# A ring of eleven places for the expert weights, 4 MB transfers from expert 2 on, and a loop over experts written out

## The reference

```python
logits = xt @ w_router + b_router            # 32 experts, top 4 of them per token
gate = softmax(top_val)
hdn = xb @ w_mlp1[e] + b_mlp1[e]             # 1024 x 2048 per expert: 8 MB
act = glu * sigmoid(1.702 * glu) * (lin + 1) # both halves clipped at 7
y   = act @ w_mlp2[e] + b_mlp2[e]            # 1024 x 1024 per expert: 4 MB
```

## Time and profile before

| | before |
|---|---|
| median of 3 runs | 1125.36 us |
| the profiled execution | 1125.41 us |
| its span | 1123.6 us |
| PE busy | 1085.1 us, 97% |
| DMA engines, weight queue | 93.3% |
| HBM read | 437.67 MB, 390 GB/s over the span |
| 4 MB transfers | 43 + 29 |
| PE waiting for weights (matmul line L1154) | 6.3 + 4.9 us |

### The profile page before, as it was taken

How to read it: one execution, slowest core, us unless ns; L and a number is a source line. 1 busy time by engine, 2 the same in 40 slices (tenths; PEclk the granted TensorE clock), 3 DMA queues, 4 the chain that set the end, 5 groups by cost and what they waited for, 6 DMA issues and landing times.

```text
span 1123.6 us, 14458 instructions
## 1 busy us (share of the span) xinstructions
PE 1085.1 (97%) x5409; PEld 487.5 (43%) x5410; DVE 367.8 (33%) x813; ACT 245.6 (22%) x345; POOL 3.6 (0%) x12
## 2 busy tenths in 40 slices
PE   9999999999999999999999999999999999999996
PEld 8888888533333333333333333333333333333332
DVE  5977787422222222222222222222222222212223
ACT  4845674311111111111111111111111111111112
POOL 0000000000000000000000000000000000000000
PEclk9999999999999999999999999999999999999999
DMA  9655469999999999999999999999999999999996
GB/s 336 223 157 165 155 204 417 428 420 416 428 427 436 430 430 429 432 428 433 435 432 395 429 433 435 433 432 432 430 429 430 433 435 432 432 432 430 426 423 253
DMA packets 37877, 439.15 MB, mean 391 GB/s; under 512 B 5244, under 2 KB 5432, under 8 KB 21880
## 3 DMA queue, kind: packets, MB, share of 16 engines
q1 hardware_dynamic: 37488, 437.78, 93.3%
q10 hardware_dynamic: 360, 0.95, 0.3%
HBM read 437.67 MB, written 1.05 MB: 390 GB/s over the span
## 4 chain that ended last, share of the span: by engine, by line
PE 79%; DMA 14%; DVE 6%; issue 0%; ACT 0%; SPq 0%; DVEq 0%; PEldq 0%; ACTq 0%
PE bank L1154 33%; PE bank L1181 18%; DMA ring<-in_w_mlp_dram 11%; PE bank L798 9%; DMA late_slots<-in_w_mlp_dram 4%; PE bank L1083 3%; PE bank L1165 2%; PE bank L792 2%; PE bank L963 2%; PE bank L1011 2%; DVE xn L1670 2%; DVE xn L1667 2%; DVE xn L1674 2%; PE bank L1059 1%; PE bank L1067 1%; PE bank L1133 1%
## 5 line engine op out<-in xcount | busy, mean ns | idle before, releaser
L1154 PE MATMUL bank<-ring,xn 128*64 128x512 f32 x1232 | 276.3, 595 | 6.3 <-DMA ring<-in_w_mlp_dram 6.3
L1154 PE MATMUL bank<-late_slots,xn 128*64 128x512 f32 x880 | 197.5, 596 | 4.9 <-DMA late_slots<-in_w_mlp_dram 4.9
L1154 PEld LDWEIGHTS bank<-ring,xn 128*64 128x64 f32 x1232 | 84.4, 136 | 163.8 <-issue 150.3
L1181 PE MATMUL bank<-ring,smo 128*64 128x512 f32 x624 | 138.3, 595 | 0.0
L705 ACT ACTIVATE xn<-bank 128x512 f32<-128x512 f32 x33 | 19.7, 598 | 481.5 <-PE bank L1154 481.5
L1154 PEld LDWEIGHTS bank<-late_slots,xn 128*64 128x64 f32 x880 | 60.2, 136 | 117.9 <-issue 106.3
L1683 DVE SCALAR_TENSOR_TENSOR moe_y_lo<-bank,st,moe_y_hi 128x512 fp32r<-128x512 f32 x33 | 24.8, 750 | 235.5 <-ACT moe_y_hi L712 235.5
L1667 DVE TENSOR_SCALAR xn<-bank 128x512 f32<-128x512 f32 x33 | 22.8, 691 | 220.9 <-PE bank L1154 220.9
L1181 PE MATMUL bank<-late_slots,smo 128*64 128x512 f32 x416 | 92.1, 595 | 0.0
L1181 PEld LDWEIGHTS bank<-ring,smo 128*64 128x64 f32 x624 | 42.9, 137 | 81.1 <-issue 81.1
L712 ACT ACTIVATE moe_y_hi<-bank,st 128x512 fp32r<-128x512 f32 x33 | 22.7, 687 | 233.7 <-PE bank L1181 233.7
(11 more groups left out here) (270 smaller groups left out, 890.9 us busy)
## 6 DMA issues: line engine op xcount, KB each, us to landing
ring<-in_w_mlp_dram SPq DMA_DIRECT2D x43, 4096.0 KB, 30.4
late_slots<-in_w_mlp_dram SPq DMA_DIRECT2D x29, 4096.0 KB, 28.0
ring<-in_w_mlp_dram SPq DMA_DIRECT2D x28, 2048.0 KB, 13.4
late_slots<-in_w_mlp_dram SPq DMA_DIRECT2D x15, 2048.0 KB, 15.6
ring<-in_w_in_dram SPq DMA_DIRECT2D x22, 1024.0 KB, 5.4
late_slots<-in_w_mlp_dram SPq DMA_DIRECT2D x8, 1024.0 KB, 38.5
ring<-in_w_branch_dram SPq DMA_DIRECT2D x4, 1024.0 KB, 5.0
ring<-in_w_out_dram SPq DMA_DIRECT2D x4, 1024.0 KB, 7.1
```

Of the source, the lines that this page charges most:

```text
L1154: last = mm(B[4 + u][g * C:(g + 1) * C, :], xgT[:, k % 4, k // 4, :], by_group(held[k // 2][0][:, k % 2, u * FF:(u + 1) * FF], g), start=F ...
L1181: last = mm(B[7][g * C:(g + 1) * C, :], actT[:, j, h * C:(h + 1) * C], held[4 + h][0][:, j // 2, (j % 2) * D + g * N:(j % 2) * D + (g + 1) ...
```

## The change

The ring has 11 places, chunk m goes to place m % 11, and none is used once. The eleventh is where `place_used_once` was; `smo` moves behind `sga` and `sgm` so that it adjoins the late slots. Two chunks go as one 4 MB transfer when their places adjoin, which is so for all even m but those with m % 11 equal to 3 or 9, from expert 2 to expert 29. The rounds are gone: SP's and PE's code has one stretch per expert. The first eleven chunks are issued at the same points as before, in another order. Chunks 3 and 5 of expert 31 come as 1 MB + 0.5 MB + 0.5 MB, and PE waits for the last 0.5 MB only before the matmuls that use it. The final scalings are put in another order. The weight of the final norm is read into another place and issued one chunk later.

```diff
-PLACES = 10
-ROUND = PLACES // 2
-QUADS = range(ROUND + 1, E - 2)
+FIRST_QUADS = 2
+PLACES = 11
+QUADS = [m for m in range(CHUNKS * FIRST_QUADS, CHUNKS * (E - 2), 2) if m % PLACES not in (3, PLACES - 2)]
...
-        late_pair = [late[:, 2 * i:2 * i + 2, :] for i in range(4)]
-        places = [late_pair[1], pair[0], pair[1], pair[4], pair[5], pair[2], pair[3], late_pair[2], late_pair[3], late_pair[0]]
+        late_pair = [late[:, 2 * i:2 * i + 2, :] for i in range(5)]
+        places = late_pair[1:5] + pair + late_pair[0:1]
+        quads = {n: late[:, at:at + 4, :] for n, at in ((PLACES - 1, 0), (0, 2), (1, 4), (2, 6))}
+        quads.update({4 + n: ring[:, 2 * n:2 * n + 4, :] for n in range(5)})
...
                 if pieces == 2:
-                    for half, done in enumerate((place_landed[place], piece_landed[i])):
-                        sp.dma_start(places[place][:, half, :], src[:, half * SLOT:(half + 1) * SLOT]).then_inc(done, 16)
+                    at = [0, SLOT, 2 * SLOT] if i % 2 == 0 else [0, SLOT, SLOT + FF, 2 * SLOT]
+                    for a, b, done in zip(at, at[1:], (place_landed[place], piece_landed[i], half_landed.get(i))):
+                        sp.dma_start(places[place].rearrange("p a n -> p (a n)")[:, a:b], src[:, a:b]).then_inc(done, 16)
...
             sp.wait_ge(p_turned, AH)
-            load(0, 0, 0)
+            first_load(0)
             sp.wait_ge(slots_used, Q_BRANCH + 2)
-            load(0, 1, 1)
-            load(0, 4, 4)
+            first_load(4)
+            first_load(9)
             sp.wait_ge(slots_used, Q_OUT)
-            load(0, 2, 2)
-            load(0, 3, 3)
+            first_load(5)
+            first_load(8)
             sp.wait_ge(mg_turned, 2 * TT)
-            load(0, 5, None)
+            first_load(3)
             sp.wait_ge(slots_used, Q_OUT + 2)
-            load(1, 0, 5)
-            load(1, 2, 7)
+            first_load(1)
+            first_load(6)
             sp.wait_ge(slots_used, Q_MOE)
-            load(1, 1, 6)
-            load(1, 3, 8)
-            load(1, 4, 9)
+            first_load(2)
+            first_load(7)
+            first_load(10)
...
-            for e in range(1, ROUND + 1):
-                refill(e, e, CHUNKS, e + 2 in QUADS, e + 1 in QUADS)
-            with sp.Fori(1, E // ROUND - 1) as r:
-                for c in range(1, ROUND + 1):
-                    refill(r * ROUND + c, c, CHUNKS, True, True)
...
+            for e in range(E - 1):
+                after = sp.value_load(first_item[0:1, e + 1:e + 2], min_val=1, max_val=ITEMS - 1)
+                for i in range(CHUNKS):
+                    m = CHUNKS * e + i + PLACES
+                    if m >= CHUNKS * E:
+                        continue
+                    if m not in QUADS and m - 1 not in QUADS:
                         wait_freed(after, i)
+                        load(m // CHUNKS, m % CHUNKS, m % PLACES, 2 if m >= CHUNKS * (E - 1) + 2 else 1)
+                    elif m - 1 in QUADS:
                         wait_freed(after, i)
+                        load_quad(m // CHUNKS, m % CHUNKS // 2, (m - 1) % PLACES)
             after = sp.value_load(first_item[0:1, E - 1:E], min_val=1, max_val=ITEMS - 1)
-            wait_freed(after, 2)
+            wait_freed(after, 3)
...
+                        if u and k == KB - 1 and 3 in in_halves:
+                            pe.wait_ge(*in_halves[3])
...
+                        if j == 3 and 4 + h in in_halves:
+                            pe.wait_ge(*in_halves[4 + h])
...
-            experts(0, chunks)
-            pe.wait_ge(opened, 2 * TT)
-            scatter_b2()
-            with pe.Fori(1, (E - 2) // ROUND) as r:
-                experts(r, lambda c: chunks_in_round(c, r))
-            with pe.Fori(last_first, items) as i:
+            after = after_first
+            for e in range(1, E - 1):
+                if e == E // 2:
+                    pe.wait_ge(opened, 2 * TT)
+                    scatter_b2()
+                first = after
+                after = pe.value_load(first_item[0:1, e + 1:e + 2], min_val=1, max_val=ITEMS - 1)
+                with pe.Fori(first, after) as i:
+                    item(i, chunks(e))
+            with pe.Fori(after, items) as i:
...
-            final_scale(0)
+            final_rstd(0)
+            final_half(0, 0)
             final_mean(1)
-            final_scale(1)
+            final_half(0, 1)
+            final_rstd(1)
+            final_half(1, 0)
+            final_half(1, 1)
```

More of the change, by code:

```diff
@@ L115, in landings @@
     for m in range(CHUNKS * E):
[L116 to L121, removed]
+        place = m % PLACES
+        if m - 1 in QUADS:
             table.append(table[-1])
@@ L158, in build @@
         xhi_at = late_at
[L159 removed]
+        late = nc.alloc_sbuf_tensor_at("late_slots", [P, 2 * HALF + 2, SLOT], F32, offset=late_at)
         xhi_room = sb("xhi_room", [P, KB, S])
@@ L1101, in chunks, with item @@
             def chunks(e):
[L1103 to L1122, removed]
+                at = [(m, *landing[m]) for m in range(CHUNKS * e, CHUNKS * (e + 1))]
+                return [(places[m % PLACES], place_landed[place], 16 * count) for m, place, count in at]
             def by_group(columns, g):
                 return columns.rearrange("p (q g s) -> p g q s", g=2, s=ROWS)[:, g]
-            def item(i, held, in_pieces={}):
+            def item(i, held, in_pieces={}, in_halves={}):
                 pe.wait_ge(row_ready, i + 1)
@@ L1184, in item @@
                     last.then_inc(slots_used, 2)
+            items = pe.value_load(first_item[0:1, E:E + 1], min_val=1, max_val=ITEMS - 1)
             with pe.Fori(0, after_first) as i:
-                item(i, [(places[n], place_landed[n], 16) for n in range(CHUNKS - 1)] + [(once[:, :, :], once_landed, 16)])
-            last_first = pe.value_load(first_item[0:1, E - 1:E], min_val=1, max_val=ITEMS - 1)
-            items = pe.value_load(first_item[0:1, E:E + 1], min_val=1, max_val=ITEMS - 1)
-            def experts(r, held):
-                after = pe.value_load(first_item[0:1, bass.ds(r * ROUND + 1, 1)], min_val=1, max_val=ITEMS - 1)
-                for c in range(1, ROUND + 1):
-                    first = after
-                    after = pe.value_load(first_item[0:1, bass.ds(r * ROUND + (c + 1), 1)], min_val=1, max_val=ITEMS - 1)
-                    with pe.Fori(first, after) as i:
-                        item(i, held(c))
-            experts(0, chunks)
-            pe.wait_ge(opened, 2 * TT)
-            scatter_b2()
-            with pe.Fori(1, (E - 2) // ROUND) as r:
-                experts(r, lambda c: chunks_in_round(c, r))
-            with pe.Fori(last_first, items) as i:
-                item(i, chunks(E - 1), {c: (piece_landed[c], 16 * (SLOTS[:Q_MOE].count(c - 2) + 1)) for c in piece_landed})
+                item(i, chunks(0))
+            after = after_first
[8 more added lines that the diff above has]
+            with pe.Fori(after, items) as i:
+                item(i, chunks(E - 1), {c: (piece_landed[c], 16 * (SLOTS[:Q_MOE].count(c - 2) + 1)) for c in piece_landed},
+                     {3: (half_landed[3], 16 * (SLOTS[:Q_MOE].count(4) + 1)), 5: (half_landed[5], 16 * (SLOTS[:Q_MOE].count(5) + 1))})
             pe.wait_ge(gT_ready, items + 1)
@@ L1696, in final_scale, with final_half @@
                 dve.wait_ge(rstd, 2 * TT + t + 1)
-                for n in range(2):
-                    cut = slice(n * N, (n + 1) * N)
-                    v.scalar_tensor_tensor(out=xn[:, t, cut], in0=B[2 * t + n][:, :], scalar=st[:, 6 + t:7 + t],
-                                           in1=wfin[:, cut], op0=ALU.mult, op1=ALU.mult).then_inc(normed, 1)
+            def final_half(t, n):
+                cut = slice(n * N, (n + 1) * N)
+                v.scalar_tensor_tensor(out=xn[:, t, cut], in0=B[2 * t + n][:, :], scalar=st[:, 6 + t:7 + t],
+                                       in1=wfin[:, cut], op0=ALU.mult, op1=ALU.mult).then_inc(normed, 1)
             dve.wait_ge(s_small2, 16)
```

39 lines of the change are left out of this document (16 added, 23 removed).

## The result

The changed kernel takes 1129.17 us (median of 8 runs, 1128.16 to 1131.54); the kernel before, run beside it, 1125.36 us (8 runs, 1124.67 to 1126.95). The ratio is 1.0035, 95% interval 1.0026 to 1.0044: it is slower. The forecast was 1126.4, no difference that can be told.

The account below looks back on a forecast made before the run. The weight queue's landings up to chunk 189, then a fixed tail, were taken to bound the kernel. Landings 2.2 - 0.8 + 0.6 + 0.2 = +2.2 and tail -1.2 gave +1.0 on 1125.41: 1126.4 us, range 1123.6 to 1128.9.

Parts of the forecast that it names:

- What bounds the kernel: Weight queue sets the end: landing of chunk 189's last piece, then a fixed tail of PE and DVE work.
- Code written out: PE code from 507 to 1101: 22 more blocks, three full rounds of eight plus part of a fourth, +2.2 us.
- My own check from the front: Landings summed from the first quad at 240.1, plus 6.3 for blocks and 0.3 for edges: 1103.5 against 1101.0.
- Slower: the blocks go on the same engines: Rival, weights' queue: dearer blocks or last round complete before 1101; +3.6 us, 1129.0, chance 0.2.
- 4 MB from expert 2 on: Early weight transfers: first quad lands at 240.1, +0.6 us; four more pairs of singles, +0.2.
- My bound for an empty queue: First quad: with an empty queue a quad lands 12.3 us after its issue, so 240.6 at most.
- Ring of eleven: One more chunk in flight from expert 1 on: -0.8 us near 250, 0 at the expert with two items.
- Half pieces: Tail, expert 31's chunk 3: four passes run while the last 0.5 MB lands, -0.9 us.
- final scalings: Tail: DVE's 0.42 us wait for the square root goes, second half's mean moves to the middle, -0.3 us.
- the cover that I named: Expert 31's tail: chunk 5's last quarter is needed 0.3 us after landing; if late, 0.5 at most is given back.
- The blocks are hidden: Rival: added code blocks delay no landing; -1.5 us, 1123.9, chance 0.2.
- The ring fills a real gap: Rival: slice 22's dip to 395 GB/s was lost time, 2.3 us come back; 1124.1, chance 0.08.

Follow-up runs that it names:

- the new end with the old code: Kernel before with only the half pieces and the new order of the final scalings: 1124.89 us, ratio 0.9995.
- two experiments: PE's code alone written out on the kernel before, 1130.0 us; 4 MB transfers from expert 6 on, on the changed kernel, 1130.17 us.
- the second profile of the same kernel: The changed kernel run again without edit, beside the kernel before on another chip: 1128.59 us, ratio 1.003.
- the kernel with less code: Kernel before with the new tail and 28 fewer PE instructions (7 warming matmuls of 512 columns for 14 of 256): 1123.82 us, ratio 0.9984.

## Why the prediction was wrong, step by step

*What bounds the kernel*: right. The landing of chunk 189's last piece and the tail behind it give the whole difference of the two profiles, +4.1 - 1.3.

*Code written out* (+2.2, ends 0 and +4.5) is **the step that failed**, and by its size. The blocks came as counted: 22 in 507 to 1101, one about every 27 us. I counted the rounds wrongly. I let the fourth be "a part", 0.6 us, since it would be complete "only around 1095, just before chunk 189 lands"; just before is before, and the block at 1097.7 cost its whole 1.2 us on the second half of chunk 188, right ahead of 189. My own check from the front shows the size: it had 6.3 us for blocks and 0.3 for edges, 6.6 together, and 7.7 were measured; with a whole fourth round (1.5) it would have been 7.5. The written-out PE code alone makes the landing +3.0 and the time +4.7 (1130.0 against 1125.25, ratio 1.0038), where I took +2.2.

The rival *Slower: the blocks go on the same engines* had the condition "or the last round is complete before 1101" and the price 1129.0, at a chance of 0.2. The condition came true, for PE's blocks; of SP's blocks nothing was seen. That its price agrees with the median to 0.2 us is in part luck: it stands for landings +4.8, measured +4.1, and the median lies 1.0 above the profiled execution.

*4 MB from expert 2 on* (+0.8): the first quad landed at 240.7 where I had 240.1; the miss is 0.6. My bound for an empty queue, 12.3 us, was not that: the quad of 600.91 was issued 2.6 us before the one ahead of it landed, at 603.5. The first quad of the changed kernel, issued 1.4 us before the landing ahead of it (230.1), landed 10.7 us after that landing, not 9.72. The pairs of singles cost 0.4 and not 0.2. A line that I read over plays a small part: PE's read of `items` moved ahead of expert 0, so PE's first weight matmul starts at 216.14 in place of 215.66, and at 215.83 with the read put back.

*Ring of eleven* (-0.8 near 250): a gain of that size isn't there. The 0.8 us of before stood around a block fetched at 251.1, and I took it for a queue that ran short. In the changed kernel the queue is fuller there (435 GB/s over 246 to 262 us, against 393), a block comes at 251.2 all the same, and the landing at 261.7 is late by 1.4. The 0.8 isn't even a fixed property of the old ring: kernels with the same ring and code are 2.2, 1.0, 2.0, 0.8 and 0.3 us over plain prices from chunk 13's landing to chunk 21's (the kernel before, then the new end with the old code and with less, PE's code all and half written out). Over the whole chain PE's written-out code with ten places is 7.9 over, the changed kernel with eleven 7.7: 0.2 is left for the place. Zero at the two-item expert was right.

The parts then add up without a rest. From before to changed the landing of the first quad gives +1.2 (240.7 against chunk 13's 239.5), five pairs more as singles +0.4, and what is over plain prices 7.7 - 5.2 = +2.5: together +4.1. Forecast for the same three were +0.6, +0.2 and 2.2 - 0.8 = +1.4. Behind 555 us alone the changed kernel is 4.7 over plain prices, the kernel before 1.4, and the pairs of singles add 0.7.

*Half pieces* and *final scalings* (-1.2): right, -1.3. From the last piece to the end of PE's last pass on chunk 189 it is 1102.61 + 3.68 - 1105.11 = 1.2 us, before 1101.01 + 1.96 - 1100.97 = 2.0; so -0.8 for -0.9 predicted. The 32 passes on chunks 4 and 5 run unbroken in 7.04 us: the cover that I named held. Half a us is from the last scalings, 0.3 predicted.

*The blocks are hidden* and *The ring fills a real gap* fell. The rule of the Trainium skill ("Runtime: NRT & Kernel Launch", Instruction fetch mechanics), by which crossing into the next block is mostly hidden and a written-out loop is preferred, agrees with the trace for the engine that fetches: items keep their 26.77 us in code that runs for the first time. For the kernel it doesn't hold: writing out PE's code alone is 0.38% slower. Two rows of the chain of waits of the changed kernel:

```profile
817.13 7.04 PE bank L1127 x32
843.90 7.04 PE bank L1127 x32
```

*Not in the prediction*: what a late landing does to PE's clock. The sum took each us of landing as a us of time. With waits of 2.0 to 3.2 us the granted clock often fell to its lower level for 3.4 or 6.8 us. In two experiments this, with starts that were late already, made PE the bound and put more time between landing and end: 24.2 us with the old end (22.6 before, so +1.6) and 24.7 with the new one (21.3, so +3.4). Before, no wait for weights was longer than 1.4 us and none had a fall behind it. In the changed kernel's profiled execution one fall came, behind 2.52 us at 1013, and it was made up by the next wait for weights. Nor did the sum have the distance from the profiled execution to the median: 0.05 us before, 1.0 changed. Where that comes from is open.

## What to carry to other kernels

In a kernel that its weight queue bounds, count the 16 KB blocks of code that come in during the bound stretch. Here the loop that repeats its code has none, and written-out code pays some 1.5 us for each eight (7.7 us over plain prices for 33 blocks), most of it in one step. A block that comes after a long stretch without any pays a full step alone (1.2 us at 1098 before, 1.1 at 1101 with the new end); so where the last one falls can matter, and 28 instructions fewer ahead moved it from 1101.0 to 1110.2, behind the last transfer that counts. With the new end this was the one version here that beats both kernels (by 0.16%; without the 28 the ratio was 0.9995, and the two intervals just overlap). When a sum puts an event "just before" the instant that sets the end, count it whole.

## What the runs showed of the hardware

The cost of code blocks comes mostly in steps: in the changed kernel's profile seven of eight blocks move no landing by more than 0.2 us, the eighth by 1.2 to 1.4, with the steps 195 to 225 us apart; with PE's code alone written out the last three are 206 us apart. In the second profile of the same kernel the same blocks cost 1.0 to 1.1 and another of each eight costs 0.4, 1.5 per eight in all. It fits that the blocks go round the engines; which engine each one hit was not tested by an experiment. With half of the code written out, and with 4 MB transfers from expert 6 on, the steps are less clean (0.4 to 1.0), and the kernel with less code has one of 2.1 without a block, so the rule is not exact.

TensorE's granted clock is at 1.2 GHz for 3.4 us at idle times of 1.97, 2.02, 2.18 (in two profiles), 2.39, 2.42, 2.52, 2.61, 2.81 and 2.83 us, and for 6.8 us at one of 3.16. Idle times of 2.17, 2.18 (twice), 2.19 and 2.38 us had no fall, and before, with 1.4 at most, there was none ahead of the tail. At one and the same wait, 2.18 us before 947.5, the second profile of the changed kernel has a fall and the first has none: the length of an idle time alone doesn't decide it.
